# Waiting tile by tile, inside the first output tile, for what a second layer reads

## The reference

```
# first block
x = x + gt1 * mixer(h)                                  # mLSTM and pooling
a = square(relu(h @ w_ff1))                             # ff1: 1024 -> 4096, in two halves of 2048
x = x + gt2 * (a @ w_ff2)                               # ff2: 4096 -> 1024, in two halves
# second block
y_ssd = ssd_mixer(z, xbc, dt) @ w_ssd_proj              # 2048 -> 1024
y_mla = attention(q, k, v) @ w_mla_proj                 # 1024 -> 1024
g_ssd, g_mla = split(sigmoid(gates + gate_b))
x = x + (g_ssd * y_ssd + g_mla * y_mla) @ w_o           # 1024 -> 1024
u = conv3(h @ w_up)                                     # 1024 -> 5632, causal, by channel
x = x + (silu(u_gate) * u_val) @ w_down                 # 2816 -> 1024
```

## Time and profile before

| | us |
|---|---|
| median of 3 runs | 1880.22 (1879.92, 1880.22, 1885.13) |
| profiled execution | 1885.22 |
| its span | 1883.3 |
| TensorE busy (matmul) | 1709.9, 91% |
| VectorE busy | 1166.7, 62% |
| ScalarE busy | 679.6, 36% |
| mean granted clock of TensorE | 0.95 |

### The profile page before, as it was taken

The page is one execution under the profiler, slowest core; times in us unless marked ns, Lnnn a source line. Parts: engine busy times, 40 slices in busy tenths (PEclk is TensorE's granted clock), DMA queues, the critical chain, the costliest instruction groups (busy, mean ns, idle before and its releaser), DMA issues.

```text
span 1883.3 us, 19773 instructions
## 1 busy us (share of the span) xinstructions
PE 1709.9 (91%) x7731; PEld 1355.1 (72%) x7731; DVE 1166.7 (62%) x1446; ACT 679.6 (36%) x956; POOL 171.9 (9%) x134
## 2 busy tenths in 40 slices
PE   3849998999999988998999999977989799989998
PEld 2737876878887866885666788855657688878886
DVE  5887676543354466787777754466755677762374
ACT  2413332221222124434777332267841233321231
POOL 0695700000000000000000000000410000000000
PEclk8969998999999989999999999997999899999999
DMA  7544131222222213221111233211002222222322
GB/s 311 199 162 159 45 117 63 90 90 102 100 90 90 93 67 136 90 89 45 46 68 45 90 113 120 89 68 45 1 21 81 77 90 90 97 82 91 111 90 89
DMA packets 25725, 176.25 MB, mean 94 GB/s; under 512 B 2849, under 2 KB 3233, under 8 KB 4897
## 3 DMA queue, kind: packets, MB, share of 16 engines
q1 hardware_dynamic: 21888, 149.66, 21.9%
q0 software_dynamic: 2304, 16.78, 2.4%
q10 hardware_dynamic: 1440, 8.55, 1.1%
HBM read 170.53 MB, written 4.46 MB: 93 GB/s over the span
## 4 chain that ended last, share of the span: by engine, by line
PE 74%; DVE 15%; ACT 6%; issue 2%; DMA 2%; POOL 2%; ACTq 0%; DVEq 0%; SPq 0%; POOLq 0%
PE bank L1370 23%; PE bank L1371 22%; PE bank L1372 22%; DVE w_lo L736 2%; ACT p L342 2%; ACT pt L342 1%; DMA ada_chunk<-ada 1%; DVE p L1117 1%; PE bank L1776 1%; ACT w_hi L342 1%; PE bank L1659 1%; PE bank L1508 1%; DVE rs L748 1%; PE bank L1490 1%; PE bank L1426 1%
## 5 line engine op out<-in xcount | busy, mean ns | idle before, releaser
L1370 PE MATMUL bank<-h,w_hi 128*128 128x512 f32 x1216 | 486.7, 400 | 53.5 <-DVE w_lo L736 23.3
L1371 PE MATMUL bank<-h,w_hi 128*128 128x512 f32 x1216 | 479.5, 394 | 0.0
L1372 PE MATMUL bank<-h,w_lo 128*128 128x512 f32 x1216 | 479.1, 394 | 0.0
L342 ACT ACTIVATE w_hi<-raw 128x2048 fp32r<-128x2048 f32 x130 | 249.2, 1917 | 418.1 <-DMA raw<-slabs 415.4
L736 DVE TENSOR_TENSOR w_lo<-raw,w_hi 128x2048 fp32r<-128x2048 f32 x130 | 305.7, 2351 | 57.8 <-ACT w_hi L342 53.2
L1370 PEld LDWEIGHTS bank<-h,w_hi 128*128 128x128 f32 x1216 | 232.3, 191 | 111.4 <-issue 39.6
L1371 PEld LDWEIGHTS bank<-h,w_hi 128*128 128x128 f32 x1216 | 232.4, 191 | 49.2 <-issue 1.0
L1372 PEld LDWEIGHTS bank<-h,w_lo 128*128 128x128 f32 x1216 | 231.9, 191 | 49.4
L1370 PE MATMUL bank<-a_hi,w_hi 128*128 128x512 f32 x432 | 172.4, 399 | 16.1 <-DVE a_lo L742 16.1
L1371 PE MATMUL bank<-a_lo,w_hi 128*128 128x512 f32 x432 | 171.8, 398 | 0.0
L1372 PE MATMUL bank<-a_hi,w_lo 128*128 128x512 f32 x432 | 171.3, 397 | 0.0
(11 more groups left out here) (323 smaller groups left out, 2387.7 us busy)
## 6 DMA issues: line engine op xcount, KB each, us to landing
raw<-slabs SPq DMA_DIRECT2D x130, 1024.0 KB, 4.9
ada_chunk<-ada POOLq DMA_DIRECT2D x16, 1024.0 KB, 5.2
ada_chunk<-ada ACTq DMA_DIRECT2D x8, 1024.0 KB, 20.1
x<-x_in SPq DMA_DIRECT2D x4, 1024.0 KB, 8.5
spill_x<-x SPq DMA_DIRECT2D x1, 2048.0 KB, 6.7
x<-spill_x SPq DMA_DIRECT2D x2, 1024.0 KB, 4.9
out<-x SPq DMA_DIRECT2D x8, 256.0 KB, 2.0
inv<-inv SPq DMA_DIRECT2D x1, 1024.0 KB, 7.7
```

The lines of the kernel that those rows point to most:

```text
L342: return act.activation(out, in_, f, **kw)
L1370: pe.matmul(out, w[0], a[0], start=start, stop=False)
L1371: pe.matmul(out, w[0], a[1], start=False, stop=False)
L1372: return pe.matmul(out, w[1], a[0], start=False, stop=stop)
```

## The change

`product` gets a parameter `made`, a semaphore and a count. In the first output tile of the layer, and only there, TensorE waits before each step k until the semaphore is at the count for tile k. The seven waits for all tiles, ahead of `product`, are gone. In the layers with `made` the wait for the first slab and the wait for the bank now come before the first wait for an input tile.

```diff
-            def product(name, hi, lo, kt=KT, slabs=None, stage=None, between=None):
+            def product(name, hi, lo, kt=KT, slabs=None, stage=None, between=None, made=None):
...
                         for k in range(kt):
+                            if t == 0 and made is not None:
+
+                                pe.wait_ge(sem(made[0]), made[1] + k + 1)
                             last = three(banks[bank0 + t % 2][:], weights(slab, (16 if wide else KT) * m + k),
                                          (hi[:, k, :], lo[:, k, :]), k == 0, k == kt - 1)
...
-                pe.wait_ge(sem("a_ready"), 16 if half == "a" else 32)
-                product("ff2" + half, a_hi, a_lo, 16)
+                product("ff2" + half, a_hi, a_lo, 16, made=("a_ready", 0 if half == "a" else 16))
...
-            pe.wait_ge(sem("ys_split"), XS_T)
...
-            product("ssd", ys_hi, ys_lo, 16, between=gain_turn)
+            product("ssd", ys_hi, ys_lo, 16, between=gain_turn, made=("ys_split", 0))
...
-            pe.wait_ge(sem("att_made"), 8)
-            product("mla", att[:, 0:16:2, :], att[:, 1:16:2, :])
-            pe.wait_ge(sem("mm_made"), 8)
-            product("wo", mm_hi, mm_lo)
+            product("mla", att[:, 0:16:2, :], att[:, 1:16:2, :], made=("att_made", 0))
+            product("wo", mm_hi, mm_lo, made=("mm_made", 0))
...
-            pe.wait_ge(sem("fa_made"), 16)
-            product("downa", a_hi, a_lo, 16)
+            product("downa", a_hi, a_lo, 16, made=("fa_made", 0))
             product("upb", h_hi, h_lo)
-            pe.wait_ge(sem("fa_made"), UP_T)
-            product("downb", a_hi, a_lo, UP_T - 16)
+            product("downb", a_hi, a_lo, UP_T - 16, made=("fa_made", 16))
```

## The result

The changed kernel takes 1851.88 us (median of 4 runs, 1850.24 to 1854.19), the kernel before 1882.68 us beside it (4 runs, 1879.92 to 1887.35). The ratio is 0.9832, 95% interval 0.9814 to 0.985: 31 us faster (28 to 35 by that interval), where 30.6 were forecast.

What follows compares the result with a forecast made beforehand. TensorE, 74% of the span, bounds the kernel, so gains come from its idle or slow time. 19.6 us idle plus 11.0 clock make 30.6, from the median 1880.22 to 1849.6, forecast 1850 us; range 1844 to 1864.

Steps and rivals of the forecast that it cites:

- The sum, 30.6 us: Gains at ff2a 4.61, ff2b 4.60, ssd 0, mla 3.79, wo 4.64, downa 8.47, downb 4.50 us, added waits 0.
- Idle time, 19.6 us: TensorE standstill removed at ff2a 2.88, ff2b 2.88, mla 2.05, wo 2.92, downa 5.48, downb 3.40 us.
- The clock, 11.0 us: Time lost to slow matmuls at the 1.2 GHz level after the stalls, expected back: 11.0 us of the gain.
- either all or nothing returns: At mla, of the 1.74 us clock loss behind the stall; all was taken, with 2.05 us idle making 3.79.
- A low clock in the first steps without a stall: Sign of being wrong: low clock in the touched layers' first output tiles although no stall stands there.
- Met waits, 0: The 86 added waits, nearly all already satisfied, cost 0 us; upper bound 0.19 us each, 16.3 us in all.
- The next slab isn't late: Weights of the next slab stay in time: 3.1 us to spare in downa, 2.5 in downb, over 5 in ff2a and wo.
- ssd, 0: At ssd the split of ys ends long before the first weight load, so nothing waits: gain 0 us.
- Downb's remaining clock loss, 1.72: In downb a stall of 2.08 us stays; 1.72 of the 2.82 us clock loss left in, 1.10 counted as gain.
- Rival 5: First step held by something else, a bank or the first slab, so TensorE starts as late: 1880 us; chance 0.03.

Runs made afterwards that it cites:

- filled stalls: Kernel before, all seven waits kept, TensorE doing matmuls nobody reads during six stalls: 1876.92 us against 1884.87, ratio 0.9956; again 1874.0 against 1883.08, ratio 0.9966.
- half filled ones: Kernel before with 6, 6, 4, 6, 12, 12 unread matmuls in the stalls of ff2a, ff2b, mla, wo, downa, downb: 1877.72 us against 1883.08, ratio 0.997.
- mla undone: Changed kernel with mla alone waiting for all eight pairs again: 1857.51 us, ratio 0.987 to the kernel before.

## Why the prediction was right

- **The sum, 30.6 us.** That it agrees with the measured 31 to under 1 us is in part luck. The interval of the gain is 28 to 35 us, and the stretches with the same code changed by 1.5 us between the two traces compared.
- **Idle time, 19.6 us.** Right at each place to 0.1 us. The step that needs the late tile comes after the tile at five places, and in downb after 2.1 us of waiting, as worked out from its six steps.
- **The clock, 11.0 us.** The mechanism is shown by the filled stalls, in three traces; that the size goes with the length of the idle time is shown by one trace of the half filled ones. The value agreed with this pair of traces (30.5 at the places for 30.6), but rested on one execution. In three traces of the kernel before the six places took 59.8, 57.1 and 58.0 us; one stall of 2.72 us lost nothing in two of the three. With their mean the forecast would have been about 1.5 lower.
- **mla, "either all or nothing returns".** This step was wrong in form. Over ten traces 2.9 us returned on average where 3.79 stood in the sum; in the pair compared it was 3.68. A low clock in the first steps without a stall was named as a sign of being wrong, and two of the five traces without the stall show some of it at mla: 3.79 and 3.95 us for fifteen steps, 3.53 to 3.55 in the others.
- **Met waits, 0.** Right: 87.04 us for 128 steps, with 128 of them and with 16.
- **The next slab isn't late.** Right: no w_lo wait in a second tile; w_lo is at 22.8 us for 23.3.
- **ssd, 0.** Right, no gap was there.
- **Downb's remaining clock loss, 1.72.** It lost 1.74 in the trace compared (tail of the layer 30.76 us for 29.02). Of five traces with this stall four lost as much; the fifth, that of mla undone, took 29.17 us. The value was right, but not as something that comes with every stall.
- Rival 5 fell with the first timeline after, where both layers shown start 0.23 us behind the last matmul of the one before.

## What to carry to other kernels

A wait for all input tiles ahead of a dense product costs the whole chain behind the last tile; a wait for each tile inside the accumulation cost nothing here and hides a chain as long as the steps ahead of the last one. Count these steps: sixteen covered 5.5 us, six did not. And price a stall of TensorE by the stretch from the last matmul before it to the point where the pitch is back, not by the idle time, in more than one trace, for the clock's part varies.

## What the runs showed of the hardware that I had not expected

- The same stall doesn't always lose the clock. 2.72 us idle at ff2b was followed by fifteen steps in 5.12 and 5.14 us in two traces and in 3.53 us in two others. 1.94 us idle in downb cost 1.7 us of clock in four traces and at most 0.2 in a fifth. Of the stalls cut to 1.36 to 1.40 us none of three lost it, of those over 5 us all six did (6.18 to 6.40 us for fifteen steps).
- The stretch ahead of ff2a, the same code in every kernel here, ended between 404.6 and 411.1 us in fourteen traces. That alone is 6.5 us, where the runs of the kernel before spread over 10.7 (1876.7 to 1887.4).
